# Hybrid encoder trunk on one core: shared weights for pairs of token units, x loaded as columns in layer 0, state-space inputs multiplied once, and three engines' queues in another order

## The reference

```python
proj = x @ w_in                                   # 1024 x 5640
r_q, r_k, r_v, r_z, s_u, s_z, m_x, m_v, m_o, m_z, m_i, m_f, a_q, a_z = split(proj)
ret = retention(r_q, r_k, r_v, positions) * silu(r_z)
s5o = s5(s_u, ...) * silu(s_z)                    # complex diagonal state space, GLU
xc  = silu(causal_conv(m_x, ml_conv_w))           # q, k by head from xc
ml  = head_norm(mlstm(q, k, m_v, m_i, m_f) * sigmoid(m_o)) * ml_gn * silu(m_z)
mk, mv = split(mem @ xa_w_kv)                     # 256 memory tokens
xa  = softmax_attention(a_q, mk, mv) * silu(a_z)
x   = layer_norm(ALPHA * x + concat(ret, s5o, ml, xa) @ w_out, ln_g, ln_b)
```

## Time and profile before

| | |
|---|---|
| median of 3 runs | 1873.7 us |
| profiled execution | 1873.72 us, its span 1871.9 us |
| PE matmul records / busy | 10992 / 1798.6 us |
| VectorE, ScalarE, GpSimd busy | 1035.0, 604.4, 522.4 us |
| DMA | 236.54 MB, mean 126 GB/s |

### The profile page before, as it was taken

How to read it: one execution, slowest core, us unless ns; L and a number is a source line. 1 busy time by engine, 2 the same in 40 slices (tenths; PEclk the granted TensorE clock), 3 DMA queues, 4 the chain that set the end, 5 groups by cost and what they waited for, 6 DMA issues and landing times.

```text
span 1871.9 us, 27041 instructions
## 1 busy us (share of the span) xinstructions
PE 1798.6 (96%) x10992; PEld 1578.5 (84%) x10992; DVE 1035.0 (55%) x2002; ACT 604.4 (32%) x853; POOL 522.4 (28%) x238
## 2 busy tenths in 40 slices
PE   5999999999999999999989999999999999999997
PEld 5878897889988998878887788978999889988786
DVE  6997615461374378339649675254613825772524
ACT  4442344431124313432243332444311242143320
POOL 2443213112121413345336232121211131134451
PEclk9999999999999999999999999999999999999999
DMA  7435355132023205674335333541410331167451
GB/s 249 150 114 142 96 188 202 46 101 70 24 68 132 94 24 209 216 272 148 101 111 167 110 101 113 192 158 57 125 34 24 107 119 68 33 244 281 148 165 52
DMA packets 99187, 236.54 MB, mean 126 GB/s; under 512 B 10864, under 2 KB 41920, under 8 KB 97784
## 3 DMA queue, kind: packets, MB, share of 16 engines
q1 hardware_dynamic: 73064, 184.25, 30.4%
q10 hardware_dynamic: 25920, 50.34, 7.3%
q0 software_dynamic: 80, 0.23, 0.0%
HBM read 171.60 MB, written 58.98 MB: 123 GB/s over the span
## 4 chain that ended last, share of the span: by engine, by line
PE 79%; DVE 8%; DMA 6%; ACT 4%; issue 2%; POOL 2%; ACTq 0%; SPq 0%; DVEq 0%
PE gp L573 19%; PE gp L575 18%; PE gp L574 18%; DMA wraw<-in_w 4%; PE mm L573 2%; PE mm L575 2%; PE mm L574 2%; DMA yraw<-yt 2%; POOL wlo L1072 2%; PE mm L785 1%; PE mm L694 1%; ACT whi L1149 1%; DVE sz L1838 1%; PE mm L763 1%; PE mm L925 1%
## 5 line engine op out<-in xcount | busy, mean ns | idle before, releaser
L1072 POOL TENSOR_TENSOR wlo<-wraw,whi 128x1024 fp32r<-128x1024 f32 x168 | 434.9, 2606 | 1152.0 <-ACT whi L1149 1151.8
L573 PE MATMUL gp<-whi,xh 128*128 128x256 f32 x1280 | 382.0, 298 | 0.0
L575 PE MATMUL gp<-whi,xl 128*128 128x256 f32 x1280 | 362.8, 283 | 0.0
L574 PE MATMUL gp<-wlo,xh 128*128 128x256 f32 x1280 | 362.5, 283 | 0.0
L573 PE MATMUL gp<-xh,whi 128*128 128x512 f32 x768 | 321.5, 419 | 5.3 <-ACT xh L1190 2.9
L575 PE MATMUL gp<-xh,wlo 128*128 128x512 f32 x768 | 302.2, 394 | 0.0
L574 PE MATMUL gp<-xl,whi 128*128 128x512 f32 x768 | 301.6, 393 | 0.0
L573 PEld LDWEIGHTS gp<-whi,xh 128*128 128x128 f32 x1280 | 245.9, 192 | 7.7 <-issue 7.5
L574 PEld LDWEIGHTS gp<-wlo,xh 128*128 128x128 f32 x1280 | 245.9, 192 | 4.8 <-issue 4.7
L1149 ACT ACTIVATE whi<-wraw 128x1024 fp32r<-128x1024 f32 x172 | 175.8, 1054 | 225.8 <-DMA wraw<-in_w 114.8
L575 PEld LDWEIGHTS gp<-whi,xl 128*128 128x128 f32 x1280 | 245.3, 192 | 0.0
(11 more groups left out here) (326 smaller groups left out, 2996.9 us busy)
## 6 DMA issues: line engine op xcount, KB each, us to landing
wraw<-in_w SPq DMA_DIRECT2D x172, 512.0 KB, 4.2
spill<-gate ACTq DMA_DIRECT2D x32, 512.0 KB, 2.6
yraw<-yt SPq DMA_DIRECT2D x32, 512.0 KB, 5.9
xr<-in_x SPq DMA_DIRECT2D x16, 512.0 KB, 9.0
xs<-xr SPq DMA_DIRECT2D x16, 512.0 KB, 5.0
ud<-gate ACTq DMA_DIRECT2D x8, 512.0 KB, 3.0
uu<-ud SPq DMA_DIRECT2D x64, 64.0 KB, 3.4
p_tab<-kd SPq DMA_DIRECT2D x64, 64.0 KB
```

What stands on the lines that cost most here:

```text
L573: nc.tensor.matmul(out, ah, bh, start=start, stop=False)
L574: nc.tensor.matmul(out, ah, bl, start=False, stop=False)
L575: return nc.tensor.matmul(out, al, bh, start=False, stop=stop)
L1072: nc.gpsimd.tensor_tensor(wlo[slot(u)][:, 1024 * i:1024 * i + 1024], wraw[n % 2], whi[slot(u)][:, 1024 * i:1024 * i + 1024].bitcast(F32), ...
```

## The change

The token units become pairs. `token_unit` runs two units of 256 columns as one of 512: the first of the pair does tokens 0 to 511 and the second tokens 512 to 1023, and each goes first over the first four k tiles (weights in slot 0) and then over the last four (slot 1). The weights of these units are stored accordingly. So both PSUM halves stay open until hook 12 and hook 16 of a unit, where they were done at 8 and 16, and ScalarE's evictions move to hook 12; slot 0 is free after hook 8 of the second unit (`w_used`), slot 1 at its end. In layer 0 x is also given transposed and loaded as columns into the place of `xl`; ScalarE and VectorE split it there, and the 64 transposes go. The constants load after the first weights. PE waits for weight halves one by one, and in the first state-space unit for x tile by tile. `s_inputs` multiplies once; `scan` takes the sine product from the other half of the partitions in two instructions and subtracts. SyncE's weight loads in the state-space units move from hook 0 to hook 5; ScalarE's splits and evictions in QK are spread over hooks; the SiLUs, projections and exponentials of `weigh` and the split for LO change places; the low halves for LO stand among GpSimd's masks. Head norms go by chunks, not by heads, `MLH` moves by two hooks with its two halves ordered by tokens, and a halving in the mLSTM's denominator becomes a doubling beforehand.

```diff
-TG, TH, TTOP = 0, 192, 320
+TG, TH, TTOP = 0, 128, 256
...
+T_PAIRS = (U_RZ, U_RV, U_LV, U_LZ, U_LO)
+T_UNITS = {u + i for u in T_PAIRS for i in range(2)}
...
-MLH = [14 + 2 * k for k in range(8)]
+MLH = [16 + 2 * k for k in range(8)]
...
+        xraw = at("xraw", KT * T, o_x + KT * T)
...
-            def x_load(half):
-                for c in range(4 * half, 4 * half + 4):
-                    sp.dma_start(xr[c], dram["x"][128 * c:128 * c + 128, :]).then_inc(xn_in[half], 16)
+            def x_load(i):
+                sp.dma_start(xraw[:, 2 * T * i:2 * T * i + 2 * T].rearrange("p (k t) -> p k t", k=2),
+                             dram["xT"][256 * i:256 * i + 256, :].rearrange("(k p) t -> p k t", p=128)).then_inc(xn_in[i], 16)
...
+            sp.dma_start(cst, dram["cst"]).then_inc(S["c_in"], 16)
             x_load(0)
             raw(0, U_MK + 1)
             x_load(1)
+            x_load(2)
+            raw(0, U_SU[0], range(1))
+            x_load(3)
+            raw(0, U_SU[0], range(1, 2))
+            sp.dma_start(rp[:, 1024:2048].bitcast(I32), bass.AP(dram["pos"].tensor, 0, [[0, 128], [1, T]])).then_inc(S["pos_in"], 16)
...
                 for w, u in enumerate(S5_UNITS):
-                    raw(l, u + 2)
                     for i in range(16):
+                        if i == 5:
+                            raw(l, u + 2)
...
+            def token_unit(l, u, fill=None):
+
+                i = u % 2
+                for kh in range(2):
+                    v = u - i + kh
+                    for c in range(4):
+                        if kh == 0 and c % 2 == 0:
+                            pe.wait_ge(g_free[c // 2], units_to(l, u) - 1)
+                        for j in range(4):
+                            if c == 0 and j % 2 == 0:
+                                pe.wait_ge(S["lo_done"], l * HALVES + half0(v) + j // 2 + 1)
+                            a0 = T * (4 * kh + j) + 128 * (4 * i + c)
+                            last = mm3(gp[c // 2][:, 512 * (c % 2):512 * (c % 2) + 512], xh[:, a0:a0 + 128], xl[:, a0:a0 + 128],
+                                       whi[kh][:, 512 * j:512 * j + 512], wlo[kh][:, 512 * j:512 * j + 512],
+                                       kh == 0 and j == 0, kh == 1 and j == 3)
+                            if kh == 1 and j == 3 and c % 2:
+                                last.then_inc(g_done[c // 2], 1)
+                            if i == 1 and kh == 0 and c == 3 and j == 3:
+                                last.then_inc(S["w_used"], 1)
+                            if fill and j % 2:
+                                fill(8 * kh + 2 * c + j // 2)
...
-                pe.wait_ge(S["lo_done"], l * HALVES + half0(u) + nhalf(u))
+
+                def weights(k):
+                    if k % 4 == 0 and k // 4 < nhalf(u):
+                        pe.wait_ge(S["lo_done"], l * HALVES + half0(u) + k // 4 + 1)
...
-                        for w in range(2):
-                            a0 = GCOLS * (GB * (b % 2) + g) + TG + 64 * w
-                            last = nc.tensor.matmul(zbank(b)[:, 256 * w + 128 * g:256 * w + 128 * g + 128], p_tab[q % 2][:, a0:a0 + 128],
-                                                    uview(b)[:, 128 * g:128 * g + 128], start=True, stop=True)
+                        a0 = GCOLS * (GB * (b % 2) + g) + TG
+                        last = nc.tensor.matmul(zbank(b)[:, 128 * g:128 * g + 128], p_tab[q % 2][:, a0:a0 + 128],
+                                                uview(b)[:, 128 * g:128 * g + 128], start=True, stop=True)
...
-                    if 6 <= hook < 22 and hook % 4 in (2, 3):
-                        m_project((hook - 6) // 4, hook % 4 - 2)
+                    if hook < 16 and hook % 4 in (2, 3):
+                        m_project(hook // 4, hook % 4 - 2)
...
-                for u in range(U_RZ + 1, U_LO + 1):
+                for u in range(U_RZ + 1, U_LO):
                     lo(l, u)
                 for c in range(NC):
+                    if c >= 6:
+                        lo(l, U_LO, (c - 6,))
                     pool.wait_ge(S["w_exp"], NC * l + c + 1)
...
+                elif u - 2 in T_PAIRS:
+                    act.wait_ge(S["w_used"], len(T_PAIRS) * l + T_PAIRS.index(u - 2) + 1)
...
+                def x_split(i):
+
+                    act.wait_ge(xn_in[i], 16)
+                    for k in (2 * i, 2 * i + 1):
+                        F(xh[:, T * k:T * k + T], xraw[:, T * k:T * k + T], ACT.Copy).then_inc(S["xT_hi"], 1)
+
                 if l == 0:
+                    x_split(0)
                     split(l, U_MK + 1)
-                keys_evict(U_MK, 0)
-                keys_evict(U_MK, 1)
-                for i in range(16):
-                    half, k = i // 8, i % 8
-                    act.wait_ge(S["xt_done"], 16 * l + i + 1)
-                    F(xh[:, T * k + 512 * half:T * k + 512 * half + 512], bank[i % 4], ACT.Copy).then_inc(S["xT_hi"], 1)
-                    if i == 3:
-                        split(l, U_SU[0])
-                    if i == 8:
-                        keys_evict(U_MK + 1, 0)
-                keys_evict(U_MK + 1, 1)
+                    keys_evict(U_MK, 0)
+                    keys_evict(U_MK, 1)
+                    x_split(1)
+                    x_split(2)
+                    keys_evict(U_MK + 1, 0)
+                    keys_evict(U_MK + 1, 1)
+                    split(l, U_SU[0])
+                    x_split(3)
+                    act.wait_ge(S["c_in"], 16)
...
-                    A.inc(F(tab[:, :, TG:TG + 128], bk, ACT.Copy))
-                    F(tab[:, :, TG + 128:TG + 192], bk[:, :, 0:64], ACT.Copy).then_inc(S["p_ev"], 1)
+                    F(tab[:, :, TG:TG + 128], bk, ACT.Copy).then_inc(S["p_ev"], 1)
...
                 for w, u in enumerate((U_QK, U_QK + 1)):
-                    if w:
-                        split(l, u + 1)
                     for i in range(16):
-                        if i == 8:
+                        attend(16 * w + i)
+                        if i == 12:
                             if w:
                                 act.wait_ge(S["x_s"], XSTEPS * l + 8)
                             evict(l, u, 0, qk[:, T * 2 * w:T * 2 * w + T], gp[0])
-                        attend(16 * w + i)
+                        if w and i == 1:
+                            evict(l, U_QK, 1, qk[:, T:2 * T], gp[1])
+                        if w and i in (4, 14):
+                            split(l, u + 1, (i // 14,))
...
-                    if 5 <= hook < 21 and hook % 4 == 1:
-                        m_silu((hook - 5) // 4)
-                    if 6 <= hook < 22 and hook % 4 in (2, 3):
-                        m_project((hook - 6) // 4, hook % 4 - 2)
-                    if 15 <= hook < 31 and hook % 2:
-                        c = (hook - 15) // 2
+                    if hook == 9:
+                        m_silu(3)
+                    if hook < 16 and hook % 4 in (2, 3):
+                        m_project(hook // 4, hook % 4 - 2)
+                    if 17 <= hook < 25:
+                        c = hook - 17
                         act.wait_ge(S["w_arg"], NC * l + c + 1)
                         F(wt[:, 512 * c:512 * c + 512], wt[:, 512 * c:512 * c + 512], ACT.Exp).then_inc(S["w_exp"], 1)
 
+                for h in range(3):
+                    m_silu(h)
                 for w, u in enumerate((U_LZ, U_LZ + 1)):
-                    split(l, u + 1)
+                    if w == 0:
+                        split(l, u + 1)
                     for i in range(16):
-                        if i == 8:
+                        if i == 12:
                             spill(l, u, 0, 4, dram["spill"][D_LZ + 2 * w], ACT.Silu)
                         weigh(16 * w + i)
+                        if w and i in (9, 11):
+                            split(l, u + 1, ((i - 9) // 2,))
...
+                zp = zbank(b)[:, 0:256].rearrange("p (g j) -> p g j", g=GB)
+                TT(z1, ct[:, :, 1:NBT], zp, ALU.mult)
+                for i in range(2):
+                    a, o = 64 * i, 64 - 64 * i
+                    last = TT(z2[o:o + 64], st[a:a + 64, :, 1:NBT], zp[a:a + 64], ALU.mult)
+                last.then_inc(S["s_gr"], 1)
                 dve.wait_ge(S["s_gr"], NBATCH * l + b + 1)
-                V.link(TT(zv[:, :, 1:NBT], z1, z2, ALU.add))
+                V.link(TT(zv[:, :, 1:NBT], z1, z2, ALU.subtract))
...
+            powers(0)
             for l in range(DEPTH):
-                for i in range(16):
-                    half, k = i // 8, i % 8
-                    x0 = T * k + 512 * half
-                    dve.wait_ge(S["xT_hi"], 16 * l + i + 1)
-                    TT(xl[:, x0:x0 + 512], bank[i % 4], xh[:, x0:x0 + 512].bitcast(F32), ALU.subtract).then_inc(S["xT_lo"], 1)
                 if l == 0:
+                    for k in range(KT):
+                        x0 = T * k
+                        dve.wait_ge(S["xT_hi"], k + 1)
```

(2 more changed lines are left out.)

218 lines of the change are left out of this document (116 added, 102 removed).

## The result

The changed kernel took 1841.4 us in the median of 4 runs (1838.3 to 1844.7), the kernel before 1874.0: a ratio of 0.9833 (95% interval 0.9814 to 0.9852). That is faster by 32.6 us, where 61.7 were forecast, and 6 us above the upper end of the range. The profiled execution has a span of 1842.1 us against 1871.9.

The account below looks back on a forecast made before the run. TensorE, busy for 96% of the span, was taken as the bound, so time is its own work plus its waits. Terms of -20.7 -12.4 -7.6 -7.0 -6.0 -2.0 -6.0 = -61.7 took 1873.7 to 1812 us, range 1797 to 1835.

Parts of the forecast that it names:

- VectorE's rotation is covered and costs nothing: State-space stage: VectorE's extra multiply per batch, at most 0.41 us, ends hooks before PE asks; 13 us without that cover.
- Token pairs: Token units: 1920 matmuls of 512 columns replace 3840 of 256, each saving 10.8 ns; -20.7 us (-18 to -24).
- second weights late: Rival: second weights late in every pair, 4.3 us wait plus 2.4 of slow clock in 10 pairs; 1879 us, 4%.
- State-space inputs once: State-space units: 64 of 128 input matmuls go, 14.2 us, with 4 x 0.45 us returned to waits; -12.4 us (-10 to -14.2).
- SyncE's order: State-space units: weight loads go behind table loads, so four output-matmul waits for late issue go; -7.6 us (-4 if landing is late).
- a table chain might hold the stage: Rival: kernel store, landing and reload hold the state-space stage, so input and SyncE terms go; 1832 us, 14%.
- The start: Layer 0's start: PE starts at 12.9, first state-space unit at 31.2 instead of 40.7, 2.3 lost to slow clock; -7.0 us.
- moves by the same 7.3: Step of the start term: VectorE's own chain, which feeds the first tables, ends x's low parts about 33.3 instead of 40.56.
- The mLSTM weights: mLSTM: SiLU waits and slow clock go (-12.8), new 3.4 us waits before the output-gate unit come (+6.8); -6.0 us (0 to -13).
- Attention: Attention: two of four waits for turned scores shrink as ScalarE's eviction and splits are spread; -2.0 us for both layers (0 to -3).
- Waits for weight halves: PE's five waits for low weight halves, 6.0 us, go by waiting half by half; -6.0 us (-3 to -6).
- The near ends: The smallest gain taken for every term, all together: -39 us, giving 1835 us, the range's upper end.

Follow-up runs that it names:

- short-angle run: Changed kernel without range reduction of the rotary angles in layer 0, the angles scaled down instead, so retention's rotation is left out: 1835.9 us, ratio 0.9797.
- masks first: Changed kernel with GpSimd's low halves for the output-gate unit (LO) placed behind all eight masks: 1834.3 us, ratio 0.9812.
- later low halves: Changed kernel with GpSimd's two low halves for the attention gate's first unit taken after the 13th and 15th recurrence steps, not together at the 12th: 1833.5 us, ratio 0.9815.

## Why the prediction was wrong

The sign, the start of TensorE and most of the waits that would go were right; the sum was twice what came. Most of the miss is one step, that VectorE's rotation is covered and costs nothing in the state-space stage (24.1 us forecast there, 6.9 came), and most of the rest lies in LZ and LO. By its own steps:

- **Token pairs, -20.7.** Right in kind. Spaced 227 ns, no wait in the middle of a pair, and no second weights late. The size was a little high: undoing three quarters of the width cost 10.8 us, 14.4 for all; the five token stages of layer 0 give 6.8 us for three quarters, which is 18 for both layers. The price from the pure rows holds in RV, which went from 48.11 to 45.62 us; where small matmuls stand between, as in LV (71.11 to 69.72), less is gained.
- **State-space inputs once, -12.4.** Failed, with SyncE's -7.6 behind it: the stage with RZ gave 6.9 in place of 24.1. The step is "its rotation ends hooks before PE asks for it, so I cost it at nothing". The cover holds only while VectorE's instructions keep their short durations, like the 0.41 us in the earlier trace rows. In the fourth round before it was 3.2 us, but zc and zs beside GpSimd's low halves last 2.4 to 2.6 us each and the scan beside its table products 2.60 in place of 0.74; with the low halves out of the way 0.55 us of cover are left there. Going back to two products cost 0.4 us as the kernel stood, within the spread, and 13.9 with GpSimd out of the way. That a table chain might hold the stage was a rival, at 1832 and 14%; it held, by the scan and not by the table's way through DRAM that the rival named.
- **SyncE's order, -7.6.** The mechanism was right: the late loads went, and come back when it is undone. But what came back into the time was some 5 us, at the edge of the spread, since the next in line was VectorE.
- **The start, -7.0.** TensorE started at 12.76 (forecast 12.9) and the first state-space unit at 34.22, where 31.2 was forecast: GpSimd's low half for it ended at 34.01. It took 3.33 us instead of 2.4 beside VectorE's split of x, and ScalarE's copy ahead of it ended at 30.6. The slow clock came as forecast, 0.50 from 34.2 to 38.8, some 2.3 us. The step that failed is that VectorE's own chain "moves by the same 7.3". It ended x's low parts at 38.55, 2.0 us earlier than before. From there to 104 us it paused once, for 1.78 us, for the DMA of p_bc at 84.18; before, this pause was 0.38 us, so that 1.4 of the 2.0 us went there, and the first outputs ran at 111.78 where they had run at 112.31. The whole start was worth half a microsecond there. The short-angle run shows that VectorE's queue is what holds them; whether GpSimd's low halves have a part in this stretch was not tried.
- **The mLSTM weights, -6.0.** The wait before the query projection fell to 0.36 us (half a microsecond forecast), and the new wait is 3.10 us (3.4 forecast). Two things were not in the sum: the half clock behind that wait, which came in layer 1 and not in layer 0, though the earlier trace rows show a slower clock behind 4.07 us in both; and the second wait of 2.35 us, behind low halves that the pairs moved to another place of the recurrence. I had checked only that those weights come in time, and not what they run beside. With the pairs' share (some 5.7 us) taken off, LZ and LO lost 3 us instead of gaining 6. The runs with masks first and with later low halves give back 7.5 and 8.3.
- **Attention, -2.0.** The four waits for pt, 7.5 us, are two of 4.5, but those for pm rose from 1.2 to 3.6: -0.6.
- **Waits for weight halves, -6.0.** They are 1.7 us now: -4.3.

The near ends together gave -39 in the prediction (its terms add up to -38), and -32.6 came. They left out a common cause: all three covers (of the sine multiply, the start, the recurrence) were VectorE's, and GpSimd's low halves act on the first and the third, as the runs show.

## What to carry to other kernels

When a change moves or adds work on VectorE or GpSimd, lay both timelines over each other and count a VectorE instruction with both operands in SBUF as ending with the GpSimd instruction beside it (here 0.42 us became 2.4 to 2.6); "hidden" then needs a cover of that length. A change of when a buffer comes free moves the work that waits for it: give that work a place where its neighbour on the other engine has slack, by a wait or another order. Three such moves on GpSimd were worth 29 us here, one of them by letting the masks go ahead of the low halves in its own queue. And a saving on the busiest engine counts only where that engine, and not its supplier, ends last.

## What the hardware showed that was not expected

- A VectorE multiply of 64 partitions takes as long as one of 128: two of 64x256 take 0.85 us, one of 128x256 takes 0.42. Splitting one by partitions doubles it.
- A delay of 0.5 us on VectorE turned into some 4 us, as zc and zs slipped behind the start of a GpSimd instruction. Even a product of two columns (128x2) took 2.38 us there, instead of 0.16.
- TensorE's granted clock stood at 0.50 for the six microseconds after waits of no more than 3.10 and 3.15 us, and at 1.00 after another wait of 3.10 us in the same profile.
